# Feed-forward down product: the 16 pair chunks as four groups of seven half-token products

## What is computed

```python
D_MODEL, SEQ, D_FF = 1024, 512, 2816

def swiglu(x, w_gate, w_up, w_down):
    return (jax.nn.silu(x @ w_gate) * (x @ w_up)) @ w_down

# first_block
h = h + 0.5 * swiglu(rms_norm(h, ffn1_norm), ffn1_w_gate, ffn1_w_up, ffn1_w_down)
...                       # two attention branches, gated, merged, projected
h = h + 0.5 * swiglu(rms_norm(h, ffn2_norm), ffn2_w_gate, ffn2_w_up, ffn2_w_down)
return rms_norm(h, final_norm)
# second_block: rmsnorm, mLSTM mixer, rmsnorm, RG-LRU mixer, rmsnorm
```

## Time and profile before

| | us |
|---|---|
| median of three runs | 1781.68 |
| the three runs | 1781.37, 1781.68, 1785.87 |
| profiled execution | 1786.98 |
| its span | 1785.2 |

### The profile page before, as it was taken

The page is one execution under the profiler, slowest core; times in us unless marked ns, Lnnn a source line. Parts: engine busy times, 40 slices in busy tenths (PEclk is TensorE's granted clock), DMA queues, the critical chain, the costliest instruction groups (busy, mean ns, idle before and its releaser), DMA issues.

```text
span 1785.2 us, 24731 instructions
## 1 busy us (share of the span) xinstructions
PE 1768.2 (99%) x9474; PEld 1508.2 (84%) x9474; DVE 1168.8 (65%) x1425; ACT 852.8 (48%) x1197; POOL 300.9 (17%) x302
## 2 busy tenths in 40 slices
PE   9999999999999999999999999999999999999997
PEld 7899999888777788889989888888888888888886
DVE  6766445543777655676545567877586677868884
ACT  5445334423555544345424455454353444566673
POOL 4022111211000002012202230200201101213333
PEclk9999999999999999999999999999999999999998
DMA  7369655345221225358737223232222222233233
GB/s 245 113 159 225 160 133 127 106 146 142 93 70 52 83 95 184 98 154 211 191 107 168 81 96 101 78 99 95 95 83 89 94 83 78 92 102 105 97 130 106
DMA packets 60758, 212.71 MB, mean 119 GB/s; under 512 B 7192, under 2 KB 9368, under 8 KB 60656
## 3 DMA queue, kind: packets, MB, share of 16 engines
q1 hardware_dynamic: 39408, 135.55, 22.9%
q0 software_dynamic: 20816, 75.33, 17.4%
q10 hardware_dynamic: 432, 0.40, 0.1%
HBM read 207.04 MB, written 2.11 MB: 117 GB/s over the span
## 4 chain that ended last, share of the span: by engine, by line
PE 93%; DMA 4%; DVE 1%; ACT 1%; issue 0%; POOL 0%; POOLq 0%; ACTq 0%; DVEq 0%
PE banks L635 23%; PE banks L637 23%; PE banks L636 23%; PE banks L752 4%; PE banks L753 4%; PE banks L754 4%; DMA mx<-matrices 4%; PE banks L851 1%; PE banks L870 1%; PE banks L894 1%; DVE w_lo L2066 1%; PE banks L1029 1%; PE banks L1031 1%; PE banks L1030 1%; ACT w_hi L1433 1%; PE banks L1057 0%
## 5 line engine op out<-in xcount | busy, mean ns | idle before, releaser
L2062 DVE TENSOR_TENSOR w_lo<-w_raw,w_hi 128x1024 fp32r<-128x1024 f32 x249 | 317.0, 1273 | 314.5 <-ACT w_hi L1327 313.4
L1327 ACT ACTIVATE w_hi<-w_raw 128x1024 fp32r<-128x1024 f32 x249 | 263.4, 1058 | 381.6 <-PE banks L637 339.0
L635 PE MATMUL banks<-u_hi,w_hi 128*128 128x512 f32 x1016 | 400.4, 394 | 0.3 <-DVE u_lo L2079 0.3
L637 PE MATMUL banks<-u_hi,w_lo 128*128 128x512 f32 x1016 | 395.8, 390 | 0.0
L636 PE MATMUL banks<-u_lo,w_hi 128*128 128x512 f32 x1016 | 395.3, 389 | 0.0
L635 PEld LDWEIGHTS banks<-u_hi,w_hi 128*128 128x128 f32 x1016 | 190.8, 188 | 41.2 <-issue 2.0
L637 PEld LDWEIGHTS banks<-u_hi,w_lo 128*128 128x128 f32 x1016 | 190.7, 188 | 40.5
L636 PEld LDWEIGHTS banks<-u_lo,w_hi 128*128 128x128 f32 x1016 | 190.9, 188 | 39.0 <-issue 0.5
L752 PE MATMUL banks<-xs_hi,w_hi 128*128 128x256 f32 x512 | 145.9, 285 | 4.6 <-DVE w_lo L2066 4.6
L753 PE MATMUL banks<-xs_lo,w_hi 128*128 128x256 f32 x512 | 145.6, 284 | 0.0
L754 PE MATMUL banks<-xs_hi,w_lo 128*128 128x256 f32 x512 | 145.6, 284 | 0.0
(11 more groups left out here) (381 smaller groups left out, 3479.0 us busy)
## 6 DMA issues: line engine op xcount, KB each, us to landing
w_raw<-weights SPq DMA_DIRECT2D x251, 512.0 KB, 3.5
mx<-matrices POOLq DMA_DIRECT2D x64, 512.0 KB, 5.7
m<-matrices POOLq DMA_DIRECT2D x64, 512.0 KB, 6.9
bias<-neighbour_bias POOLq DMA_DIRECT2D x8, 384.0 KB, 4.9
v_win<-v_a POOLq DMA_DIRECT2D x16, 128.0 KB, 5.1
out_t<-x SPq DMA_DIRECT2D x16, 128.0 KB, 1.8
x<-x_t SPq DMA_DIRECT2D x3, 512.0 KB, 6.8
nm<-gate_rows POOLq DMA_DIRECT2D x4, 256.0 KB, 4.2
```

Source lines behind the costliest of these rows:

```text
L635: nc.tensor.matmul(o, wh, hi, start=start and k == 0, stop=False)
L637: ins = nc.tensor.matmul(o, wl, hi, start=False, stop=stop and k == len(pairs) - 1)
L1327: nc.scalar.activation(w_hi[:, n.slot, :], w_raw[:, n.slot, :], ACT.Copy).then_inc(hi_ready, 1)
L2062: nc.vector.tensor_tensor(w_lo[:, n.slot, :], w_raw[:, n.slot, :], w_hi[:, n.slot, :].bitcast(F32), ALU.subtract)\
```

## The change

**The down product of the pair chunks.** Its 16 hidden chunks are taken as two blocks of 8 (pairs 0 to 3, pairs 4 to 7), and the 8 output chunks as two halves. That gives four groups (`N_DOWN` = 4), each a 2 by 2 block product like a pair's: 4 output chunks, 8 hidden chunks, two halves of the tokens, seven products of 24 matmuls of 256 columns. They stand as groups 8 to 11 behind the pairs 0 to 7 in the same hand-written order, so `SP_SEQ` grows from 56 to 84 products and runs without a break. The two down parts with plain columns behind the first are gone, their weight units with them; the down weights of the pairs come through `load_matrices`.

**The operands.** The hidden values of the pairs are kept in fp32 in `hid_f` and not split when made. For each block of 8 chunks DVE makes four block sums (`block_sum`), and the seven operands in `u_hi`, `u_lo`, `xs_hi`, `xs_lo` are overwritten one by one (`refill_high` on ACT, `refill_low` on DVE) as soon as the product of group 7 (of group 9 for the second block) that read the old content has run.

**The results.** The seven products of a down group are not snapped and combined; DVE adds the bank onto a quarter of `x` after each product (`x_read`, 128x512), and PE waits for that add (`x_added`) before it adds the next product onto the same bank.

**The next norm.** The chunks of `x` are final in pairs: 0 to 3 after product (3, 10), 4 and 5 after (3, 11), 6 and 7 after (4, 11), the last product of all. `two_chunks` on ACT then makes `u_hi` and the squares of two chunks at a time.

```diff
-DOWN_PARTS = (range(0, F_PLAIN), range(F_PLAIN, 14), range(14, F_CHUNKS))
+N_DOWN = 4
+N_GR = N_SP + N_DOWN
...
-    for p in range(1, N_SP - 2):
+    for p in range(1, N_GR - 1):
         seq += [(1, p + 1), (5, p + 1), (4, p), (3, p), (6, p + 1), (2, p + 1), (7, p + 1)]
-    p = N_SP - 1
-    return seq + [(1, p), (5, p), (4, p - 1), (6, p), (3, p - 1), (7, p), (2, p), (4, p), (3, p)]
+    return seq + [(3, N_GR - 1), (4, N_GR - 1)]
...
+                if p in (N_SP, N_SP + 2):
+                    pe.wait_ge(combo_lo, refilled(f, (p - N_SP) // 2, k))
...
+                if k in (3, 4, 6, 7) and p >= N_SP:
+                    pe.wait_ge(x_added, reads(f, {3: 5, 4: 7, 6: 1, 7: 6}[k], p))
...
-                down_columns(f, 0, u0, g0)
-                for j in range(DOWN1_AFTER + 1):
+                down_plain(f, u0, g0)
+                for j in range(N_PROD):
                     pair_product(f, j)
-                down_columns(f, 1, u0, g0)
-                for j in range(DOWN1_AFTER + 1, N_PROD):
-                    pair_product(f, j)
-                down_columns(f, 2, u0, g0)
...
+                def two_squares(m):
+                    act.wait_ge(sq_added, 27 + 2 * m)
+                    nc.scalar.activation(sq[:, m % 2, :], x[:, m, :], ACT.Square, scale=EPS ** 0.5).then_inc(sq_ready, 1)
+                    nc.scalar.activation(sqb[:, m % 2, :], x[:, m, :], ACT.Square,
+                                         scale=vecs[:, V_FINAL + m:V_FINAL + m + 1]).then_inc(sq_ready, 1)
...
+                mat_high(N_PROD - 2)
+                act.wait_ge(m_used, N_PROD * f + SP_LAST_IN[0] + 1)
+                split_raw(Lin(u_next))
+                two_chunks(0, 3, N_GR - 2)
+                mat_high(N_PROD - 1)
+                two_chunks(2, 3, N_GR - 2)
+                act.wait_ge(m_used, N_PROD * f + SP_LAST_IN[1] + 1)
+                split_raw(Lin(u_next + 1))
+                two_chunks(4, 3, N_GR - 1)
+                two_chunks(6, 4, N_GR - 1)
...
+                def x_read(j):
+                    k, p = SP_SEQ[j]
+                    if p >= N_SP:
+                        ran(k, p)
...
+                        nc.vector.scalar_tensor_tensor(dst, o[:, :].rearrange("p (c t) -> p c t", c=2), factor, dst,
+                                                       ALU.mult, ALU.add).then_inc(x_added, 1)
...
+                for j in range(SP_AT[1, N_SP + 1], SP_AT[2, N_GR - 1] + 2):
+                    mat_low(j)
+                    x_read(j - 3)
+                    block4(j - 4)
+                    refills(j)
+                    if j == SP_AT[6, N_SP + 1]:
+                        block_sum(T1, 1)
+                    if j == SP_AT[2, N_SP + 1]:
+                        block_sum(T3, 1)
+                    if j == SP_AT[7, N_SP + 1]:
+                        block_sum(T2, 1)
```

More of the change, by code:

```diff
@@ L66 @@
 U_ALL = U_END
-G_FFN = 2 * F_PLAIN + 3 * DC
+G_FFN = 2 * F_PLAIN + DC
 G_FFN1 = 0
@@ new lines, in refills, with square @@
+                def refills(j):
+                    for k, p in (SP_SEQ[j - 5], SP_SEQ[j - 4]):
+                        if p in (N_SP - 1, N_SP + 1) and (k == 4) == ((k, p) == SP_SEQ[j - 5]):
+                            refill_high(k, (p - N_SP + 1) // 2)
+                def square(m):
+                    act.wait_ge(sq_added, 9 * q_next + m)
+                    nc.scalar.activation(sq[:, m % 2, :], x[:, m, :], ACT.Square).then_inc(sq_ready, 1)
+                def two_squares(m):
[3 more added lines that the diff above has]
+                                         scale=vecs[:, V_FINAL + m:V_FINAL + m + 1]).then_inc(sq_ready, 1)
@@ new lines, in two_chunks @@
+                def two_chunks(m, k, p):
+                    act.wait_ge(x_added, reads(f, k, p))
+                    for c in (m, m + 1):
+                        g = vecs[:, gcol + c:gcol + c + 1] if f == 0 else gg[:, c:c + 1]
+                        nc.scalar.activation(u_hi[:, c, :], x[:, c, :], ACT.Copy, scale=g).then_inc(u_hi_ready, 1)
+                    for c in (m, m + 1):
+                        if f == 0:
+                            square(c)
+                        else:
+                            two_squares(c)
@@ L2195, in combo_sum, with pairs_low @@
                     nc.vector.scalar_tensor_tensor(combo(xs, k), left, -1.0, right, ALU.mult, ALU.subtract).then_inc(xs_sum, 1)
-            def pairs_low(f, u0, g0):
-                down = [u0 + 2 * F_PLAIN + DC * part for part in range(3)]
-                g_down = [g0 + 2 * F_PLAIN + DC * part for part in range(3)]
+            def pairs_low(f, u0, g0, nu_next, gcol, g_next):
+                down, g_down, u_next = u0 + 2 * F_PLAIN, g0 + 2 * F_PLAIN, u0 + U_FFN
                 def mat_low(j):
@@ new lines, in refills, with block4 @@
+                def refills(j):
+                    for k, p in (SP_SEQ[j - 5], SP_SEQ[j - 4]):
+                        if p in (N_SP - 1, N_SP + 1) and (k == 4) == ((k, p) == SP_SEQ[j - 5]):
+                            refill_low(k, (p - N_SP + 1) // 2)
+                def block4(j):
+                    k, p = SP_SEQ[j]
+                    if k == 4 and p in (N_SP - 1, N_SP + 1):
+                        block_sum(T4, (p - N_SP + 1) // 2)
+                def x_read(j):
+                    k, p = SP_SEQ[j]
+                    if p >= N_SP:
+                        ran(k, p)
+                        row, half, factor = {1: (0, H1, 0.5), 2: (0, H1, 0.5), 6: (0, H2, 0.5), 3: (0, H2, 0.5),
+                                             7: (1, H2, -0.5), 5: (1, H2, -0.5), 4: (1, H1, -0.5)}[k]
+                        o = bank[SP_BANKS[{2: 1, 5: 2, 3: 2}.get(k, 0)][p % 2]]
+                        dst = x_block(p, row, half)
+                        nc.vector.scalar_tensor_tensor(dst, o[:, :].rearrange("p (c t) -> p c t", c=2), factor, dst,
+                                                       ALU.mult, ALU.add).then_inc(x_added, 1)
@@ new lines, in pairs_low @@
+                    up_second(p)
+                    hid_second(p)
+                for j in range(SP_AT[1, N_SP + 1], SP_AT[2, N_GR - 1] + 2):
+                    mat_low(j)
+                    x_read(j - 3)
+                    block4(j - 4)
+                    refills(j)
+                    if j == SP_AT[6, N_SP + 1]:
[4 more added lines that the diff above has]
+                        block_sum(T2, 1)
@@ L2322, in pairs_low @@
-                hid_second(p)
-                split_lo(Lin(down[2] + 1))
-                pair_low(p)
+                x_read(N_PROD - 4)
+                for m in range(2, 4):
+                    u_lo_chunk(nu_next, Lin(m), gcol, g_next)
+                x_read(N_PROD - 3)
+                x_read(N_PROD - 2)
+                split_lo(Lin(u_next + 1))
+                for m in range(4, 6):
+                    u_lo_chunk(nu_next, Lin(m), gcol, g_next)
+                x_read(N_PROD - 1)
+                for m in range(6, 8):
+                    u_lo_chunk(nu_next, Lin(m), gcol, g_next)
@@ L3123, in load_matrices @@
                 a11(3)
-                for p in range(1, N_SP - 1):
+                for p in range(1, N_GR - 1):
                     s3(p + 1)
@@ L3282, in ffn @@
             columns(up_w, c)
-        for rows in DOWN_PARTS:
-            for c in range(DC):
-                columns(down_w, c, rows)
+        for c in range(DC):
+            columns(down_w, c, range(F_PLAIN))
     order = np.concatenate([np.arange(HD * h, HD * (h + 1)) for j in range(4) for h in (j, j + 4)])
```

339 lines of the change are left out of this document (174 added, 165 removed).

## The result

The changed kernel takes 1788.6 us (median of 10 runs, 1786.8 to 1790.5), the kernel before 1781.6 (10 runs on the same chip, 1780.7 to 1785.9). The ratio is 1.0036, with a 95% interval of 1.0026 to 1.0045. The change costs 7 us where the prediction had a gain of 3, and the time lies above the range of 1771 to 1788. The profiled execution took 1789.26 us, its span is 1787.4.

What follows compares the result with a forecast made beforehand. PE, busy 1768.2 of 1785.2 us, was taken to bound the kernel. Matmuls -12.9, break -4.4 and +14.3 for switches and both ends gave -3.0: 1778.7 us, own range 1775 to 1783, with rivals 1771 to 1788.

Steps and rivals of the forecast that it cites:

- matmuls: Each feed-forward part: 384 matmuls of 512 columns gone, 672 of 256 columns added; gain 12.9 us in all.
- break in the pairs: Pairs behind the middle down part: late loads make PE wait and lose clock; 6.3 us profiled, 4.4 gained in the median.
- switches, (7, 9) and (7, 11): Operand switches: DVE's backlog in group 8 makes (7, 9) wait 0.3 us per feed-forward part, 0.6 in all.
- end of f = 0: Norm behind the first feed-forward part: sum's split ends at T + 8.0, PE wants it at T + 8.2; taken 0.5 us.
- end of f = 1: Double norm behind the second feed-forward part: POOL's 16 adds cost 11.5 us of wait, 1.7 of clock; 13.2 (9.0 to 17.5).
- the 3 us at the copy of chunk 6: End of f = 1: PE wants chunk 6's copy at T + 4.1, gets it at about T + 7.
- A floor derived from the end of the chain: End of f = 1: POOL's adds end at T + 15.4, the sum's split at T + 16.9; at least 7.3 us of wait.
- The first, no collisions: POOL's adds run at 1.29 us, ends cost 9.0 us, switches and f = 0 nothing: 1771.5 us; chance 0.15.
- The third, full exclusion: POOL or DVE always blocks: f = 1 costs 17.5 us, split of (4, 11) late by 1, switches 2: 1785 us; chance 0.17.
- The load rival: Groups 5 to 11: loads don't keep up, waits recur at 0.77 us a group, clock behind some: 1797 us; chance 0.13.
- the signs of being wrong: Wrong if statistics come without a wait, waits on `w_lo` recur in groups 8 to 11, or the clock falls elsewhere.

Runs made afterwards that it cites:

- c_noadds: Changed kernel with POOL's adds of squares behind f = 0 and f = 1 on one column instead of 512, output not the reference's: 1771.8 us, ratio 0.9949.
- b_again2: The kernel before the change, unedited, profiled once more as a second execution on another chip: 1781.6 us.
- c_sums: Changed kernel with the first two block sums of the second group block moved on DVE to behind the split of (3, 8): 1785.1 us, ratio 1.0018.
- c_queue: Changed kernel, block sums and squares earlier, split of (4, 11) and adds of (2, 11), (7, 11) ahead of low parts of u chunks 1 to 3: 1779.4 us.

## Why the prediction was wrong

The ledger against the median, with what the traces and runs show in each place:

| term | predicted | measured |
|---|---|---|
| matmuls | -12.9 | -13.3 |
| break in the pairs | -4.4 | -0.8 (0 to -1.2) |
| one wait on `hid_lo` ahead of a down column, gone | 0 | -0.3 |
| switches, (7, 9) and (7, 11) | +0.6 | +3.7 |
| end of f = 0 | +0.5 | +5.5 (3.75 and 1.7 of clock) |
| end of f = 1 | +13.2 | +13.1 (4.7 + 3.9, and 4.4 of clock) |
| sum | -3.0 | +7.9 |

The runs have +7.0. The waits and clocks are those of single executions, and the changed kernel's took 0.6 us more than its median. Clock terms are length times what the granted clock lacks, less what falls into a wait. The forecast is 10 us off: 5.0 at the end of f = 0, 3.6 at the break and 3.1 at the switches; the other terms, and what the sum is above the runs, take 1.7 of it back.

*Matmuls: right.* Beside three waits that both have (1.1, 0.6 and 0.6 us), c_noadds has 5.9 us left (5.3 on adds, 0.6 on the first low part of `u`), b_again2 2.4 (1.2 on `w_lo`, 0.9 on the first low part of `u`, 0.3 on `hid_lo`). 1771.8 - 5.9 = 1765.9 against 1781.6 - 2.4 = 1779.2 is 13.3 us, for 12.9 worked out from the distance of starts.

*The break: mechanism right, size wrong.* No load wait is left, and groups 5 to 11 kept up as said. But the term was read from one execution 5.3 us above the median. I scaled 6.3 down to 4.4 by taking the middle; that the waits and their clock (6.3) are more than the whole excess (5.3) should have set it to about 1.

*The switches: mechanism right, size wrong.* The place, (7, 9) waiting for the add of (6, 9), was right in both parts, 1.47 and 1.66 us instead of 0.3. The walk chained DVE's work from (1, 9) on as if every matrix was there; DVE idled 2.29 us for one, because an add into `mx` is issued behind one of DVE's own splits. c_sums shows what the two sums cost by standing behind that idle time.

*The end of f = 0: the step that failed.* I walked ACT, POOL and the sum's split up to T + 8.0 (T is the end of (4, 11)), and the statistics of f = 0 have indeed no wait. I checked the low part of (4, 11) against its start, but not the other thing that (4, 11) waits for, the add of (7, 11), which stands on DVE four low parts of `u` behind. With plain durations it is there in time (c_noadds has no wait there), and with an earlier place it is there in time in spite of the collisions (c_queue); this order and the collisions with POOL's adds together made it 3.75 us late. I had priced collisions only for what they do to POOL, the engine that I took to be the path. They are paid on both sides, and DVE paid more: 8.7 us in f = 1 against POOL's 3.8.

*The end of f = 1: right in sum, by parts that differ.* 11.5 us of wait and 1.7 of clock were forecast, 8.7 and 4.4 came. POOL's 16 adds took 26.6 us in one row, inside the 23 to 31, and lost 3.8 us where I took 4.2. But half of the wait stands at (4, 11), where I had none, and is then missing at the statistics; the 3 us at the copy of chunk 6 did not come at all. Without its wait (4, 11) would have ended at 1028.25 + 2.88 = 1031.13, and PE would have wanted the statistics 9.6 us later; it started them at 1051.18, 10.4 us late (8.7 of wait and 1.7 of the clock), against the 11.5 that I had from POOL's row. A floor derived from the end of the chain (POOL's row cannot end sooner) was safe against a wait put at the wrong place; in f = 0 there was no such floor, and the same missed wait came on top. That the whole term agrees within 0.1 us is luck: the delay is 1.1 us smaller and the clock lost behind the statistics 1.0 larger than forecast.

*The rivals.* The first, no collisions, is out by the stretched rows above; its 1771.5 us also took the 6.3 us of the profiled execution from the median. The third, full exclusion, had the mechanism and 1785 us. It put the split of (4, 11) late by 1 us, and it was late by 0.7; it did not have the add behind the low parts, which came later still. The Trainium skill, SBUF — State Buffer, section "Who interferes with whom", has DVE instructions with two SBUF inputs contend with GpSimd instructions that read SBUF, and those with at most one not. The trace agrees on both counts (1.4 to 3.50 us for two low parts, 0.68 us always for the add with a PSUM input). The load rival is out: no wait on `w_lo`. Of the signs of being wrong one came: the clock fell in f = 0, where the forecast had no wait.

## What to carry to other kernels

When work is packed closer, walk through every semaphore that the critical engine's instruction waits for, not only the one that was close before, and do it with the stretched durations wherever two engines collide; a collision is priced on both engines. When a term is read from one execution that lies above the median, compare its size with that excess first: if they are alike, most of it isn't in the median. An in-order queue with idle time is a place: moving two block sums of DVE into 2.3 us of idle time gave 3.5 us, moving two chunks' squares of ACT into 4.7 us gave 6.6, and with these, the adds onto `x` ahead of the low parts and one of POOL's two sums on DVE, a loss of 0.4% became a gain of 0.5%.
